# Feed-forward up units of a three-layer fp32 network: the tokens' high and low parts moved as one product of 512 columns

## What is computed

```python
def conv_ffn(h, w_up, conv_w, conv_b, w_down):
    T = h.shape[1]
    a, b = jnp.split(h @ w_up, 2, axis=-1)
    a_pad = jnp.pad(a, ((0, 0), (CONV_WIDTH - 1, 0), (0, 0)))
    a = sum(a_pad[:, j:j + T] * conv_w[j] for j in range(CONV_WIDTH)) + conv_b
    return (jax.nn.silu(a) * b) @ w_down
```

## Time and profile before

| | |
|---|---|
| median of 3 runs | 898.44 us |
| profiled execution: span from the first to the last instruction | 896.5 us |
| what lies around the span, against the median | 1.94 us |
| TensorE busy | 890.7 us, 99% |
| VectorE (DVE) busy | 648.0 us, 72% |
| ScalarE (ACT) busy | 491.7 us, 55% |
| GpSimd (POOL) busy | 44.0 us, 5% |
| HBM read | 158.18 MB |
| granted TensorE clock | 1.000 |

### The profile page before, as it was taken

One profiled execution on the slowest core, in us unless ns is written; L12 is line 12 of the kernel. 1 busy time (PEld: TensorE's weight loads), 2 busy tenths in 40 slices (PEclk: granted clock), 3 DMA queues, 4 the chain that ended last, 5 costly groups with the idle time before them and its releaser, 6 DMA issues.

```text
span 896.5 us, 18673 instructions
## 1 busy us (share of the span) xinstructions
PE 890.7 (99%) x7875; PEld 864.5 (96%) x7875; DVE 648.0 (72%) x1190; ACT 491.7 (55%) x843; POOL 44.0 (5%) x50
## 2 busy tenths in 40 slices
PE   8999999999999999999999999999999999999998
PEld 7999999999999998889999999999988999999998
DVE  6987657877767789785887777677678586565664
ACT  6763555564545567575565546457437464444451
POOL 2000001000000000000000001001132000000000
DMA  8743343565465544633555653654152255555541
GB/s 320 289 180 109 136 156 139 223 225 205 148 229 189 184 152 171 242 112 108 219 185 218 230 201 147 234 190 160 37 228 95 94 212 212 192 185 209 203 154 48
DMA packets 26002, 160.68 MB, mean 179 GB/s; under 512 B 3008, under 2 KB 4928, under 8 KB 7360
## 3 DMA queue, kind: packets, MB, share of 16 engines
q1 hardware_dynamic: 25344, 158.45, 48.5%
q10 hardware_dynamic: 576, 1.05, 0.4%
HBM read 158.18 MB, written 1.05 MB: 178 GB/s over the span
## 4 chain that ended last, share of the span: by engine, by line
PE 97%; DVE 1%; DMA 1%; SPq 0%; issue 0%; ACT 0%
PE ps L412 95%; PE ps L428 2%; DMA raw<-in_w 1%; DVE arena L1716 0%; DVE wl L1266 0%; DVE arena L1700 0%; SPq L2564 0%; DVE arena L1772 0%; DVE arena L1791 0%; DVE xt L1462 0%; DVE wl L1482 0%; DVE arena L1713 0%; ACT wh L2209 0%; DVE arena L1695 0%; DVE arena L1709 0%
## 5 line engine op out<-in xcount | busy, mean ns | idle before, releaser
L1266 DVE TENSOR_TENSOR wl<-raw,wh 128x1024 fp32r<-128x1024 f32 x280 | 329.3, 1224 | 124.6 <-ACT wh L2065 124.3
L412 PE MATMUL ps<-xh,wh 128*128 128x256 f32 (+1 forms) x1264 | 352.6, 279 | 0.4 <-DVE wl L1482 0.4
L412 PE MATMUL ps<-xl,wh 128*128 128x256 f32 (+1 forms) x1264 | 350.3, 277 | 0.0
L412 PE MATMUL ps<-xh,wl 128*128 128x256 f32 (+1 forms) x1264 | 350.3, 277 | 0.0
L2065 ACT CAST wh<-raw 128x1024 fp32r<-128x1024 f32 x280 | 277.0, 1048 | 118.5 <-PE ps L412 106.4
L412 PEld LDWEIGHTS ps<-xh,wh 128*128 128x128 f32 x1264 | 237.5, 188 | 2.3 <-issue 1.1
L412 PEld LDWEIGHTS ps<-xl,wh 128*128 128x128 f32 x1264 | 237.5, 188 | 0.1
L412 PEld LDWEIGHTS ps<-xh,wl 128*128 128x128 f32 x1264 | 237.5, 188 | 0.0
L412 PE MATMUL ps<-fl,wh 128*128 128x256 f32 x528 | 145.9, 276 | 0.0
L412 PE MATMUL ps<-fh,wl 128*128 128x256 f32 x528 | 145.9, 276 | 0.0
L412 PE MATMUL ps<-fh,wh 128*128 128x256 f32 x528 | 145.9, 276 | 0.0
(11 more groups left out here) (249 smaller groups left out, 1052.4 us busy)
## 6 DMA issues: line engine op xcount, KB each, us to landing
raw<-in_w SPq DMA_DIRECT2D x144, 1024.0 KB, 4.9
raw<-in_w ACTq DMA_DIRECT2D x4, 256.0 KB, 5.3
xt<-in_x SPq DMA_DIRECT2D x4, 256.0 KB, 6.8
raw<-in_w SPq DMA_DIRECT2D x4, 256.0 KB, 8.2
arena<-in_mem SPq DMA_DIRECT2D x1, 1024.0 KB, 8.5
out<-xt SPq DMA_DIRECT2D x8, 128.0 KB, 1.9
arena<-in_sel SPq DMA_DIRECT2D x3, 256.0 KB, 5.7
small<-in_small SPq DMA_DIRECT2D x1, 623.0 KB, 6.4
```

The source lines that it names most:

```text
L412: return pe.matmul(out, lhsT, rhs, start=start, stop=stop, skip_group_check=True)
L1266: v.tensor_tensor(L[:, s], src[:, s], f32(H[:, s]), ALU.subtract).then_inc(*w_lo.up(split(i, a)))
```

## The change

From unit 5 on in f0 and unit 4 on in f1 and f2 (`APART`), up units are computed by a new function `unit_p`. It takes one product of 256 columns (low weights, high tokens) and one of 512 columns (high weights; high and low tokens side by side). The sums of wh xl then stand in columns 256 to 511 of a bank of their own for each half, so a unit takes two neighbouring banks instead of one. ACT copies those columns of both banks to SBUF (`half`), DVE adds the others to them (`parts_in`), and the two scalings read SBUF. High and low buffers of each operand become one buffer, so that one access pattern reaches both; other buffers move. The meta sums move in f1 from behind d4 to between u3 and u4, with their squares and variance. Cut to its core:

```diff
+APART = {"f0": 5, "f1": 4, "f2": 4}
...
-    CW = 8 * T + 48
+    XKG, XG, CG, FG = T + TM + 112, 8 * XW + 128, 8 * T + 128, 4 * T + 128
...
-    xkh_ = sb("xkh", T + TM, F32R)
-    rst_ = sb("rst", 48)
-    sb("gap1", 64)
-    xkl_ = sb("xkl", T + TM, F32R)
-    xh_ = sb("xh", 8 * XW, F32R)
-    meta_ = sb("meta", 8 * NM)
-    xl_ = sb("xl", 8 * XW, F32R)
+    xkhl_ = sb("xkhl", 2 * XKG, F32R)
+    sb("gap1", 16)
+    xhl_ = sb("xhl", 2 * XG, F32R)
     sb("gap2", 16)
-    coh_ = sb("coh", CW, F32R)
-    sb("gap3", 80)
-    col_ = sb("col", CW, F32R)
-    sb("gap4", 16)
-    fh_ = sb("fh", 4 * T, F32R)
+    chl_ = sb("chl", 2 * CG, F32R)
+    fhl_ = sb("fhl", 2 * FG, F32R)
     arena = sb("arena", ARW)
-    fl_ = sb("fl", 4 * T, F32R)
...
+    xkhl, xhl, chl, fhl = v3(xkhl_[:, :], XKG), v3(xhl_[:, :], XG), v3(chl_[:, :], CG), v3(fhl_[:, :], FG)
...
+    XHL = lambda c: xhl[:, :, XW * c + NM:XW * c + TM]
+    XKHL = lambda c: xkhl[:, :, TM * c:TM * c + T]
...
+    SV = arena[:, ARW - 2564:ARW - 1540]
...
-    banks = [ctx.enter_context(nc.psum_tensor(f"ps{i}", [128, 512], F32)) for i in range(8)]
+    twin = [ctx.enter_context(nc.psum_tensor(f"ps{i}", [128, 1024], F32)) for i in (0, 2)]
+    banks = [twin[i // 2][:, i % 2 * 512:(i % 2 + 1) * 512] for i in range(4)] + [
+        ctx.enter_context(nc.psum_tensor(f"ps{i}", [128, 512], F32)) for i in range(4, 8)]
+
+    def parted(b, k):
+
+        return twin[b // 2][:, :].rearrange("p (j k t) -> p j k t", j=2, k=2)[:, :, k, :]
...
+        def unit_p(name, ready, two=None):
+
+
+            i = U[name]
+            H, L = v3(wslot(wh, i), 256), v3(wslot(wl, i), 256)
+            at = (name, name + ".b")
+            P = [ps.open(n, bank_a()) for n in at]
+            for c in range(8):
+                t.wait_ge(*w_low(i, c // 4))
+                t.wait_ge(*ready(c))
+                if two and c < 2:
+                    t.wait_ge(*x_two.at(TWO[two]))
+                x = XKHL(c) if two and c < 2 else XHL(c)
+                for j in range(2):
+                    o = slice(j * 128, (j + 1) * 128)
+                    if c == 0:
+                        t.wait_ge(*ps.vacant(at[j]))
+                    mm(P[j][:, 0:T], L[:, c, o], x[:, 0, :], c == 0, False)
+                    last = mm(v3(P[j][:, :], T), H[:, c, o], x, False, c == 7)
+                    if c == 7:
+                        last.then_inc(*ps.full(at[j]))
+            used[i] = ps.ready(at[1])
...
+            up(3, tag)
+            if tag == "f1":
+                meta_sums(bank_b())
+            up(4)
             down(tag, 0)
-            unit_f(f"{tag}u5", bank_a(), XH, XL, x_in, tag)
+            up(5, tag)
             down(tag, 1)
...
+            def parts_in(f):
+                name, S = f"{tag}u{f}", v3(SV[:, f % 2 * 512:f % 2 * 512 + 512], T)
+                y, b, a = yb[f % 2][:, 0:T], yb[f % 2][:, T:2 * T], ab[f % 2]
+                d.wait_ge(*f_s.at(part(f)))
+                v.tensor_tensor(S, parted(ps.place[name][0], 0), S, ALU.add).then_inc(*ps.freed(name))
+                if f >= 2:
+                    d.wait_ge(*f_l.at(k0 + f - 2))
+                d.wait_ge(*ps.done(name))
+                v.tensor_tensor(y if cw is None else a[:, 2:2 + T], S[:, 0, :], rs, ALU.mult).then_inc(*f_a.up(k0 + f))
+                v.tensor_tensor(b, S[:, 1, :], rs, ALU.mult).then_inc(*ps.freed(name + ".b"))
...
+            def half(f):
+                if f < APART[tag]:
+                    return
+                name = f"{tag}u{f}"
+                a.wait_ge(*ps.ready(name))
+                a.wait_ge(*ps.ready(name + ".b"))
+                if f >= APART[tag] + 2:
+                    a.wait_ge(*ps.done(f"{tag}u{f - 2}.b"))
+                s.copy(v3(SV[:, f % 2 * 512:f % 2 * 512 + 512], T), parted(ps.place[name][0], 1)).then_inc(*f_s.up(part(f)))
...
-                for step in (tap0, silu, high):
+                for step in (half, tap0, silu, high):
```

More of the change, by code:

```diff
@@ L216, in program @@
     cst = sb("cst", NCN)
+    meta_ = sb("meta", 8 * NM)
+    rst_ = sb("rst", 48)
+    xkhl, xhl, chl, fhl = v3(xkhl_[:, :], XKG), v3(xhl_[:, :], XG), v3(chl_[:, :], CG), v3(fhl_[:, :], FG)
+    xh_, xl_ = xhl[:, 0, 0:8 * XW], xhl[:, 1, 0:8 * XW]
+    coh_, col_ = chl[:, 0, :], chl[:, 1, :]
+    fh_, fl_ = fhl[:, 0, :], fhl[:, 1, :]
     xt = v3(xt_[:, :], T)
@@ L393, in w_low, with parts @@
         return w_lo0.at(QUART.index((i, 2 * half + 1))) if i < 2 else w_lo.at(split(i, half))
+    def parts(tag):
+        part = lambda f: sum(22 - APART[n] for n in ("f0", "f1", "f2")[:MIX[tag]]) + f - APART[tag]
+        return part
     used = {}
@@ L617, in down, with meta_sums @@
             used[i] = ps.ready(f"{tag}acc7")
-        def meta_sums():
-            P = ps.open("sums_meta", bank_a())
+        def meta_sums(bank):
+            P = ps.open("sums_meta", bank)
             t.wait_ge(*ps.vacant("sums_meta"))
@@ L629, in ffn, with up @@
             x_in = entered(tag)
-            unit_f(f"{tag}u0", bank_a(), XH, XL, x_in)
-            unit_f(f"{tag}u1", bank_a(), XH, XL, x_in)
+            def up(f, two=None):
+                name = f"{tag}u{f}"
+                if f >= APART[tag]:
+                    unit_p(name, x_in, two)
+                else:
+                    unit_f(name, bank_a(), XH, XL, x_in, two)
+            up(0)
+            up(1)
             sums(tag, bank_b())
-            unit_f(f"{tag}u2", bank_a(), XH, XL, x_in, tag)
+            up(2, tag)
             norm_spread(tag, bank_b(), rst_)
-            unit_f(f"{tag}u3", bank_a(), XH, XL, x_in, tag)
-            unit_f(f"{tag}u4", bank_a(), XH, XL, x_in)
+            up(3, tag)
+            if tag == "f1":
+                meta_sums(bank_b())
+            up(4)
             down(tag, 0)
-            unit_f(f"{tag}u5", bank_a(), XH, XL, x_in, tag)
+            up(5, tag)
             down(tag, 1)
             for p in range(2, 10):
-                unit_f(f"{tag}u{2 * p + 2}", bank_a(), XH, XL, x_in, tag if tag == "f1" and p == 5 else None)
-                unit_f(f"{tag}u{2 * p + 3}", bank_a(), XH, XL, x_in)
+                up(2 * p + 2, tag if tag == "f1" and p == 5 else None)
+                up(2 * p + 3)
                 down(tag, p)
-                if tag == "f1" and p == 4:
-                    meta_sums()
             down(tag, 10)
@@ L1372, in ffn @@
             ab = [AB[:, 0:T + 2], AB[:, T + 2:2 * (T + 2)]]
-            rs = rs_[:, 0:T]
+            rs, part = rs_[:, 0:T], parts(tag)
             if cw is not None:
@@ L1419, in gated @@
                 d.wait_ge(*f_act.at(k0 + f))
-                d.wait_ge(*ps.done(f"{tag}u{f}"))
+                d.wait_ge(*ps.done(f"{tag}u{f}" + ".b" * (f >= APART[tag])))
                 v.tensor_tensor(b, y, b, ALU.mult).then_inc(*f_b.up(k0 + f))
@@ L1435, in ffn @@
             for p in range(11):
+                if tag == "f1" and p == 1:
+                    variance("sums_meta", rst_[0:NM, 10:11], ps["sums_meta"][0:NM, 0:1])
                 if p:
@@ L2145, in ffn @@
             ab = [AB[:, 0:T + 2], AB[:, T + 2:2 * (T + 2)]]
+            part = parts(tag)
+            def half(f):
+                if f < APART[tag]:
+                    return
+                name = f"{tag}u{f}"
+                a.wait_ge(*ps.ready(name))
[3 more added lines that the diff above has]
+                s.copy(v3(SV[:, f % 2 * 512:f % 2 * 512 + 512], T), parted(ps.place[name][0], 1)).then_inc(*f_s.up(part(f)))
             def tap0(f):
@@ L2177, in ffn @@
                     casts(f"{tag}u{2 * p + 1}", 2)
-                for step in (tap0, silu, high):
+                if tag == "f1" and p == 0:
+                    a.wait_ge(*d_meta.at(0))
+                    a.wait_ge(*ps.ready("gates"))
+                    s.activation(mq2, meta_[:, :], ACT.Square).then_inc(*s_sq.up(SQ["meta"]))
+                for step in (half, tap0, silu, high):
                     step(2 * p)
@@ L2184, in ffn @@
                     a.wait_ge(*s_meta.at(0))
-                    last = s.copy(v3(xh_[:, :], XW)[:, :, 0:NM], v3(metag, NM))
+                    last = s.copy(v3(xh_, XW)[:, :, 0:NM], v3(metag, NM))
                     last.then_inc(*x_hi.up(ENTER["meta"]))
-                    s.activation(mq2, meta_[:, :], ACT.Square).then_inc(*s_sq.up(SQ["meta"]))
             casts(f"{tag}d10", 2)
```

10 lines of the change are left out of this document (5 added, 5 removed).

## The result

The changed kernel takes 918.25 us (median of 4 runs, 918.04 to 919.33) against 898.48 us for the kernel before on the same chip: a ratio of 1.0221 [1.0208, 1.0233], slower by 19.8 us. The forecast was 894.0 us and its range ended at 899.6.

The account below looks back on a forecast made before the run. TensorE's own product step was taken to bound the feed-forward nets; -5.7 us for fewer products and +1.2 us at the ends gave -4.5 us, a forecast of 894.0 us, range 889.0 to 899.6.

Parts of the forecast that it names:

- Term (1): TensorE, split up units: three products become two, extra fixed at 6.6 ns per product; 6.7 ns less per triple, 5.7 us off.
- my bound of 13.3: Bound in ns on the long product's extra in split up units, if it grows with the columns; gain then 0.
- rival B: Split up units: the extra belongs to the columns, a pair takes 340 ns as before; 899.6 us, chance 0.12.
- Rival C: Split up units: long product slowed by reading tokens from two places, 346.6 ns a triple; 905.2 us, chance 0.08.
- (2): Split up units: ACT's added copies (31 us) and DVE's added adds (36 us) cost nothing in the steady part.
- (4): Meta sums moved to between units 3 and 4 of f1, same instructions once each: zero.
- (5): Split units take two banks of four; DVE frees one within 2 us and two units last 10.7: zero.
- (6): Moved buffers keep their start modulo 64 columns: nothing, with a risk of 4 ns per product in the range.
- Term (3): Ends of f0 and f1: a chain about 1.2 us longer costs 0.6 us each, 1.2 us on; f2 nothing.
- the long step: Sign in split up units: long product's step, 220 ns expected; 216 means A, 227 rival B, more Rival C.
- A: Split up units: loads were the limit, long product's extra only 2.6 ns, 9.1 us go; 890.5 us, chance 0.30.
- D: Split up units: more than A, by lost small waits or bare column rate, 13.3 us; 886.3 us, chance 0.06.

Follow-up runs that it names:

- e12: e2 with the 512-column product put back only in unit 6 of each net (one in f0, two in f1, four in f2); 913.1 us.
- e4: Changed kernel with the long product streaming 512 adjacent columns of the attention's buffer instead of tokens in two places; 918.2 us, 1.0217.
- e8: Changed kernel with the order of short and long product turned round in every second block; 906.62 us, 1.0093.
- e1: Changed kernel with every up unit computed by three products of 256 columns, moved buffers and meta sums kept; 898.44 us, 0.9997.
- e7: Changed kernel with the low-weight product made 512 columns too; 1013.65 us, 1.1284.
- e2: Changed kernel with the 512-column product cut in two of 256, copies, adds and banks kept; 901.31 us, 1.0028.
- e14: e2 with the last two up units of each net unsplit, without added copy and add; 898.5 us, 0.9998.
- e11: Changed kernel with both products of the split units at 320 columns, the other columns left out; 867.58 us.
- e10: Changed kernel with both products of the split units at 384 columns, the other columns left out; 909.7 us.
- e13: e2 with the long product back in one unit per net, and two token chunks of f0's unit 6 read from their second copy; 902.65 us, 1.0046.
- e6: e2 with the long product back in one unit per net, and a single-column fp32 product before each other split unit; 914.02 us, 1.0175.

## Why the prediction was wrong

**Term (1), TensorE's step, failed, and in sign.** The step of the prediction was "I read the extra as fixed per product". From two lengths 16 columns apart I took the slope to be that of the columns. Those two rows can't tell a fixed extra from one that grows with the length, since 16 columns more would add only some 0.4 to 0.7 ns to it. A long product in a stream that is still fast measures 226 ns (e12), not 220: its extra is 12.7 ns, that of two products of 256, and the pair takes the 340 of the three. That is my bound of 13.3 and rival B, at 0.12. One missing load and start gave nothing back, so the 5.7 us off were never there. In the changed kernel the long product measures 235, beyond the whole list of bounds; what carries it there is the second term. Rival C had about this price (233.3 and 346.6 ns), and e4 refutes its reason, two places; that its figures lie so near is luck.

**A second term was missing, and it makes the kernel slower.** I costed each product by itself. The runs show that the step of a 256-column product depends on what ran before it: 113.3 or 117.8 ns, same code, same addresses. A single long product leaves the slower one behind (e12), the short-long order keeps it up, e8's order doesn't. In the changed kernel this takes the pair from 340 to 353.3 ns (848 x 13.3 ns = 11.3 us) and the down units from 340 to 353.3 (6.6 us). The earlier trace rows may have held a sign of it: token-major units of 256 columns at 118 ns. I filed them under unhappy addresses and kept 4 ns per product as a risk of the moved buffers. e1 shows that those moves cost nothing. Where the 118 ns there come from wasn't tested.

**The Trainium skill**, "TensorE: Matmul & The Clock Gate", section "Back-to-back issue gap", gives two figures for 512 columns: 216 ns for a product by itself, and 131 ns per product in a sustained stream with weight loads. The runs agree with neither: 226 ns (e12) is 10 above the first and 233 (e7) 17, and the second lies below the 213.3 ns that the columns take at the granted clock. Its rule on loads from Part 3, which the prediction set aside by the trace, gains nothing here either: dropping 848 loads gave no time back.

**Terms (2), (4), (5), (6) held.** DVE's and ACT's added 36 and 31 us are hidden in the steady part, and no up unit waits for a bank: e2 less its ends is the time of before (e14), with the copies, adds, banks and moved sums in it. e1 isolates the moved sums and buffers at 0.9997.

**Term (3), the ends, was right in mechanism and short in size**: 1.47 and 1.44 us, not 0.6 each. Down 10 was released by DVE's low part as told, for 0.57 us in place of 0.3, since the chain is 1.48 us longer and not 1.2; and lateness passed into the layer behind, which I had only as the upper bound of 1.2 each, and which went beyond it. f2 cost nothing, as told.

**The sum as it is**: 901.3 (e2, which holds the ends) + 0 (length, by e12's first pair) + 11.3 (slow step, in the pairs) + 6.6 (slow step, in the down units) = 919.2, against 918.25. Of the 1.0 too much, some 0.4 is down 10's wait, which at the slower step is 0.35 us and not 0.57 in both nets. Another 0.4 is in the four units that read second copies, which grow by 0.1 us each and not by 0.2. The rest is within what these runs tell apart.

Of the signs that the prediction named, the long step was decisive: it was said that more than 227 ns means slower. And no version of this idea that was run beats the kernel before: e1 and e14 equal it, and neither has a long product. The two orders that were run throughout give 346.6 and 353.3 ns for a pair, where three products cost 340; even the first pair of e12, in a fast stream, only equals them. Two sums of the prediction are slightly off and change nothing: A without its ends is 889.3 us, not 889.0, and D's 16 ns a triple are 13.6 us, not 13.3.

**What stays open.** What in the hardware makes the two steps isn't shown. The runs show what starts the slower one (one 512-column product, e12; streams of 320 and in part of 384 columns, e11 and e10) and three things with which it ended: operands at another start modulo 64 columns (e13), the second small fp32 product though not the first (e6), and in the changed kernel the wait ahead of down 10 of f0, though not the equal one in f1. So one rival stands: that whatever shifts the time between the products and their loads can start or end the slow step, and the length is only one way to do it. Which property of a long product matters, and why long-long-short-short leaves at 340 what short-long leaves at 353.3, wasn't tried further.

## What to carry to other kernels

Merging two products that share their weights removes a load and an instruction, and neither was worth anything here: the load was already covered, and the merged product stepped like its two halves. Measure the step at the new length before the merge is built, in a stream with the real loads and order, and not by extrapolating from two lengths close together. Then look at the step of products that the edit doesn't touch: 16.9 of 19.8 us here came with the slower step of the whole stream, over a third of it in down units that have no merged product. And where a chain of engines feeds the last unit before a dependency, count handovers, and expect the whole added latency to show there, whatever the steady part hides.

## What was not expected of the hardware

- A float32r product with its own 128x128 load steps at 111.4 ns for 128 columns, 113.3 for 256, 173.3 for 384 and 226 for 512 in a fast stretch, and at 117.8, 146.7, 174.7 to 176.7 and 233 to 235 for 256, 320, 384 and 512 in a slow one, all at full granted clock: the price above the columns grows with the length (6.6 ns at 256, 12.7 at 512).
- The same 256-column product has two steps, 113.3 and 117.8 ns, and the stream keeps either for over 100 us. One product of 512 columns tipped it (e12); down 9 of f0 starts at 323.86 us there and at 319.09 in e2, 4.8 us later for that one product.
- Order matters where counts don't: the same 848 pairs cost 11.6 us less as long-long-short-short than as short-long (906.62 against 918.25).
- A product of one fp32 column in such a stream costs 0.23 us (e6), for two records of the trace: as much as two products of 256 columns.
